# The first feed-forward block in Strassen's form, the bias tables in the mixer's projection, and a new order of vector work in the tails

## The reference

```python
def swiglu(x, w_gate, w_up, w_down):
    return (jax.nn.silu(x @ w_gate) * (x @ w_up)) @ w_down

for layer in range(DEPTH):
    g = norm_gains[layer]
    x = x + FFN_RESIDUAL * swiglu(rms_norm(x, g[0]), ffn_w_gate[layer, 0], ffn_w_up[layer, 0], ffn_w_down[layer, 0])
    xn = rms_norm(x, g[1])
    x = x + (dilated_pool_mixer(xn, rel_bias, ...) if layer % 2 == 0 else mlstm_mixer(xn, ...))
    x = x + FFN_RESIDUAL * swiglu(rms_norm(x, g[2]), ffn_w_gate[layer, 1], ...)
```

## Time and profile before

| | |
|---|---|
| median of 3 runs | 2024.57 us (2024.17 to 2025.17) |
| the profiled execution | 2022.4 us, of which its span is 2020.7 us |
| feed-forward 0 on PE | 10.15 to 377.95 us |
| even mixer | 377.95 to 563.13 us |
| feed-forward 1 | 563.13 to 911.77 us |
| feed-forward 2 | 911.77 to 1267.3 us |
| odd mixer | 1267.3 to 1669.4 us |
| feed-forward 3 | 1669.4 us to the end |
| busy: PE, DVE, ACT, POOL | 98%, 68%, 41%, 24% |

### The profile page before, as it was taken

How to read it: one execution, slowest core, us unless ns; L and a number is a source line. 1 busy time by engine, 2 the same in 40 slices (tenths; PEclk the granted TensorE clock), 3 DMA queues, 4 the chain that set the end, 5 groups by cost and what they waited for, 6 DMA issues and landing times.

```text
span 2020.7 us, 27444 instructions
## 1 busy us (share of the span) xinstructions
PE 1982.1 (98%) x11114; PEld 1701.4 (84%) x11114; DVE 1364.1 (68%) x1742; ACT 836.8 (41%) x1197; POOL 492.4 (24%) x358
## 2 busy tenths in 40 slices
PE   7999999999999999998999999999998999999999
PEld 6888888876789999987999998877775788999997
DVE  6333333545498888867888886784468857988884
ACT  5323223425563433345444334554545344433331
POOL 1202112133232211223221122254025512212211
PEclk9999999999999999999999999999999999999999
DMA  5233223421132323322333333222200133333323
GB/s 178 94 99 100 94 94 116 166 84 47 58 106 94 105 94 110 100 86 90 107 105 94 106 93 110 97 85 82 81 1 1 65 103 102 97 105 105 104 90 98
DMA packets 66377, 189.23 MB, mean 94 GB/s; under 512 B 6480, under 2 KB 14928, under 8 KB 66256
## 3 DMA queue, kind: packets, MB, share of 16 engines
q1 hardware_dynamic: 66256, 187.52, 28.8%
HBM read 182.78 MB, written 4.72 MB: 93 GB/s over the span
## 4 chain that ended last, share of the span: by engine, by line
PE 85%; DVE 9%; ACT 2%; issue 2%; POOL 1%; DMA 1%; SPq 0%; DVEq 0%; POOLq 0%; ACTq 0%
PE BANKS L538 13%; PE BANKS L539 13%; PE BANKS L540 13%; PE BANKS L626 9%; PE BANKS L628 9%; PE BANKS L627 9%; PE BANKS L676 4%; PE BANKS L677 4%; PE BANKS L678 4%; PE BANKS L970 1%; DVE LO L1546 1%; DVE LO L1457 1%; DVE XC L1858 1%; PE BANKS L798 1%; DVE SQ L1914 1%
## 5 line engine op out<-in xcount | busy, mean ns | idle before, releaser
L1457 DVE TENSOR_TENSOR LO<-RING,HI 128x1024 fp32r<-128x1024 f32 (+1 forms) x136 | 177.4, 1305 | 331.9 <-ACT HI L1032 331.8
L538 PE MATMUL BANKS<-XH,HI 128*128 128x512 f32 x896 | 352.4, 393 | 15.1 <-DVE XL L1466 15.0
L539 PE MATMUL BANKS<-XL,HI 128*128 128x512 f32 x896 | 350.3, 391 | 0.0
L540 PE MATMUL BANKS<-XH,LO 128*128 128x512 f32 x896 | 350.2, 391 | 0.0
L2063 POOL TENSOR_TENSOR TMP<-TMP,RSTD 128x512 f32<-128x512 f32 x66 | 101.4, 1537 | 625.3 <-ACT TMP L1126 625.3
L1032 ACT ACTIVATE HI<-RING 128x1024 fp32r<-128x1024 f32 (+1 forms) x144 | 150.1, 1043 | 216.5 <-DMA RING<-gu_dram 89.4
L538 PEld LDWEIGHTS BANKS<-XH,HI 128*128 128x128 f32 x896 | 169.3, 189 | 56.6 <-DVE LO L1457 11.0
L540 PEld LDWEIGHTS BANKS<-XH,LO 128*128 128x128 f32 x896 | 169.0, 189 | 35.8
L539 PEld LDWEIGHTS BANKS<-XL,HI 128*128 128x128 f32 x896 | 169.3, 189 | 34.5
L626 PE MATMUL BANKS<-BF,ASH 128*128 128x256 f32 x672 | 190.8, 284 | 4.0 <-DVE ASL L1573 3.9
L628 PE MATMUL BANKS<-BF,ASL 128*128 128x256 f32 x672 | 190.2, 283 | 0.0
(11 more groups left out here) (254 smaller groups left out, 4709.3 us busy)
## 6 DMA issues: line engine op xcount, KB each, us to landing
RING<-gu_dram SPq DMA_DIRECT2D x176, 512.0 KB, 3.4
DRAW<-down_dram SPq DMA_DIRECT2D x32, 512.0 KB, 3.8
RING<-oin_dram SPq DMA_DIRECT2D x32, 512.0 KB, 3.4
RING<-down_dram SPq DMA_DIRECT2D x32, 384.0 KB, 3.2
RING<-down_dram SPq DMA_DIRECT2D x16, 512.0 KB, 3.4
RING<-ein_dram SPq DMA_DIRECT2D x16, 512.0 KB, 3.4
RING<-oout_dram SPq DMA_DIRECT2D x16, 512.0 KB, 3.4
DRAW<-down_dram SPq DMA_DIRECT2D x16, 384.0 KB, 3.6
```

What stands on the lines that cost most here:

```text
L538: pe.matmul(PS[bank][:], HI[j][:, c], hi(k), start=(n == 0), stop=False)
L539: pe.matmul(PS[bank][:], HI[j][:, c], lo(k), start=False, stop=False)
L540: last = pe.matmul(PS[bank][:], LO[j][:, c], hi(k), start=False, stop=(n == len(order) - 1))
L1457: dve.tensor_tensor(LO[j][:, 0:kt * P], RAW[j][:, 0:kt * P], HI[j][:, 0:kt * P].bitcast(F32), ALU.subtract).then_inc(lo_ready, 1)
```

## The change

Feed-forward 0 is now a `block_ffn` as well, with `PLAIN` 4, `LATE` 6 and `EARLY` 16 as feed-forward 1 has them, so four plain pairs and 18 blocks; `ffn` and `walk_ffn` are gone. It begins with `start_of_program` in place of `start_of_stage`: units 0, 1, and unit 2 with the norm inside. Its forms are made right behind the start, the first of them ahead of the squares' low part. The bias tables move to the even mixer's input projection: heads 0 and 1 behind unit 3, then two heads behind each of the units 4, 5 and 6. Their table inputs `HOT` and `RELB` are loaded at the end of feed-forward 0; `STG` lies in two halves in another region, each half with a write of its own. In all the tails of `block_ffn` the low part of the weights of tile m - 1 stands between the add and the low part `XL` of tile m.

```diff
-PLAIN = (None, 4, 3, 3)
+PLAIN = (4, 4, 3, 3)
-LATE = (None, 6, 7, 7)
+LATE = (6, 6, 7, 7)
...
# SP
+                if f == 0:
+                    sp.wait_ge(early_done, EARLY)
+                    sp.dma_start(RELB[:], relb_d).then_inc(hot_in, 16)
+                    sp.dma_start(HOT[:], hot_d).then_inc(hot_in, 16)
+                    sp.dma_start(PICK[:], pick_d).then_inc(prep_in, 16)
+                    sp.dma_start(POOLW[:], poolw_d).then_inc(prep_in, 16)
...
-            ffn(0, Q_FFN[0], ein_d)
-
-            sp.wait_ge(skew_out, 16)
+            block_ffn(0, Q_FFN[0], ein_d)
+            for n in range(4, 11):
+                load(Q_EIN + n // 4, n % 4, ein_d[n if n < 8 else 8 + (n - 4) % 8])
+            for n in range(2):
+
+                sp.wait_ge(bias_staged, HA * (n + 1))
+                sp.dma_start(skew_d[4 * n:4 * n + 4].rearrange("h p z -> p h z"), STG[n][:]).then_inc(skew_out, 16)
+            for n in range(11, 13):
+                load(Q_EIN + n // 4, n % 4, ein_d[n if n < 8 else 8 + (n - 4) % 8])
+            sp.wait_ge(skew_out, 32)
...
# PE, start of the program and the even mixer
+            def start_of_program():
+
+                unit(0, 0, KX, xh, xl, ready=x_tile_ready(0))
+                unit(0, 1, KX, xh, xl)
+                unit_with_norm(0, 0)
...
                 start_of_stage(q0, 1)
                 unit(q0, 3, KX, xh, xl)
+                bias_table(0)
+                bias_table(1)
                 for j in range(SLOTS):
                     unit(q0 + 1, j, KX, xh, xl)
+                    if j < 3:
+                        bias_table(2 * j + 2)
+                        bias_table(2 * j + 3)
...
# ACT, even mixer
+                act.wait_ge(hot_in, 32)
+                act.activation(HOTR[:], HOT[:], ACT.Copy).then_inc(bias_ready, 1)
+                act.activation(RBH[:], RELB[:], ACT.Copy).then_inc(bias_ready, 1)
+
+                def staged(h):
+                    for n, (z0, z1) in ((2 * h, (0, T)), (2 * h + 1, (T, BW))):
+                        act.wait_ge(bias_sum, n + 1)
+                        act.activation(STG[h // 4][:, h % 4, z0:z1], PS[5 + n % 3][:, 0:z1 - z0],
+                                       ACT.Copy).then_inc(bias_staged, 1)
+
                 for n in range(12):
                     if n < 8:
                         act.wait_ge(bank_free, N_EIN + n + 5)
                         act.activation(SQB[:, n, :], QK[:, n, :], ACT.Square).then_inc(qk_sq, 1)
                     split_unit(N_EIN + n + 4)
+                    if 3 <= n <= 6:
+                        staged(2 * n - 6)
+                        staged(2 * n - 5)
...
# DVE, tails
-                for m in range(KX):
-                    residual_tile(q0 + (NU + m) // 4, m % 4, r, m, 0.5)
+
+                def split_behind(m):
                     if m < 4:
                         split(NU + 4 + m, late)
                     elif after:
                         split(NU + 4 + m, whole)
+
+                for m in range(KX):
+                    residual_add(q0 + (NU + m) // 4, m % 4, m, 0.5)
+                    if 1 <= m < KX - 1:
+                        split_behind(m - 1)
+                    if after:
+                        new_x_tile(r, m)
                     if f == 1:
                         forms_behind(2, m)
+                split_behind(KX - 2)
+                split_behind(KX - 1)
```

More of the change, by code:

```diff
@@ L196, in trunk @@
         HL = at("HL", [P, 8, T], hr0, 8 * TB, F32R)
[L198 to L201, removed]
+        STG = [at(f"STG{n}", [P, HA // 2, BW], hr0, 8 * n * TB) for n in range(2)]
+        HOT = at("HOT", [P, BW], hr0, 6 * TB)
+        HOTR = at("HOTR", [P, BW], hr0, 6 * TB, F32R)
+        RELB = at("RELB", [P, HA], hr0, 15 * TB // 2)
         QK = at("QK", [P, 8, T], e0, 0)
@@ L376, in early_loads @@
         def early_loads(f, p):
-            before = sum(len(early_pieces(i, n)) for i in range(1, f) for n in range(PLAIN[i], PLAIN[i] + EARLY))
+            before = sum(len(early_pieces(i, n)) for i in range(f) for n in range(PLAIN[i], PLAIN[i] + EARLY))
             return before + sum(len(early_pieces(f, n)) for n in range(PLAIN[f], p + 1))
@@ L383, in x_order @@
         def x_order(r):
-            return PAIRED if r >= 3 else tuple(range(KX))
+            return tuple(range(KX)) if r in (0, 2) else PAIRED
         NU = 2 * FT
-        def is_gate_up(lq, last):
-            return lq < (3 if last else 4)
         block = ctx.enter_context(nc.Block())
@@ L406, in load_half @@
                              src[:, :, first:first + 4 * P].rearrange("m p c -> p m c")).then_inc(weights_in[j], 16)
[L408 to L420, removed]
-                            load(q, j, gu_d[f, 32 + 4 * (lq + 1) + j] if lq + 1 < 3
-                                 else down2_d[f, 4 * (lq - 2) + j])
-                        elif lq + 1 < 4:
-                            load(q, j, gu_d[f, third * 16 + (4 * (lq + 1) + j)])
-                        elif lq + 1 < 6:
-                            load(q, j, down_d[f, third * 8 + (4 * (lq - 3) + j)])
-                        else:
-                            load(q, j, gu_d[f, third * 16 + (16 + j)])
-                walk_ffn(sp, step)
             def block_ffn(f, q0, after):
@@ L1642, in block_ffn @@
                 whole, right = slice(0, KMAX * P), slice(4 * P, KMAX * P)
-                now, first, late = (2, 3, 5)[f - 1], PLAIN[f], slice(0, LATE[f] * P)
-                if f == 1:
+                now, first, late = GAIN_OF[f], PLAIN[f], slice(0, LATE[f] * P)
+                if f < 2:
                     form(f, 0)
```

169 lines of the change are left out of this document (35 added, 134 removed).

## The result

The changed kernel takes 2042.66 us (2041.89 to 2044.69) against 2024.37 us (2021.57 to 2025.17) of the kernel before: a ratio of 1.0094, with a 95% interval of 1.0077 to 1.0112. The forecast was 2037 us, from 2030 to 2045. The profiled execution of the changed kernel takes 2042.0 us with a span of 2040.3, so it is 19.6 us longer than that of before.

A forecast was written before the change was run, and what follows sets the result against it. PE, busy 98% of the span, was taken to bound the kernel by its work plus waits. Terms -13.9 + 5.6 + 20.4 + 5.0 - 4.4 = +12.7 on 2022.4 gave 2035.1, with the median 2.2 above: 2037 us, range 2030 to 2045.

The forecast's parts named there:

- Blocks and start: Feed-forward 0: 18 blocks save 14.4 us, the start costs 2.9; -13.9 us in all, including 5.6 of bias tables leaving.
- The wait at the norm: Start of feed-forward 0: PE waits 0.8 us for the norm's sums, because the first form precedes the squares' low part.
- The loads of the tables' inputs: About 1.1 MB loaded ahead of the mixer's first weights: costed at nothing, up to 2 us if the cover is gone.
- The form by itself: Feed-forward 0 in Strassen's form, without the leaving bias tables: a gain of 8.3 us.
- Table waits: Mixer's projection: bias parts wait for ACT's copies, 7.8 us behind unit 3, 4.2 behind units 4, 5, 6; +20.4 us.
- Bias matmuls: The bias tables' matmuls leave feed-forward 0 and come back in the even mixer: +5.6 us.
- The clock: Even mixer: PE's granted clock falls in the 7.8 us wait and most 4.2 us ones; +5 us, between 1.7 and 7.
- The tail: Feed-forward 1's tail in the new order: the 4.35 us wait at feed-forward 2's start shrinks; -4.4 us, between 0 and -6.1.
- Rival 1: Table waits as forecast, but the clock falls once and the tail gives 6.1: +7.7, 2032 us; chance 0.85 together with the forecast.
- Rival 2: Mixer's projection: copies keep up with PE, so bias parts find banks free; -12.7, 2012 us; chance 0.06.
- Rival 3: Feed-forward 0: DVE stays behind, up to 5 us, clock falls there and at each table wait (+4); some 2046 us; chance 0.06.

The follow-up runs named there:

- four banks: Bias parts in four banks instead of three, with ACT's copies ahead of the square and split, against the changed kernel: 2012.16 us, ratio 0.9942.
- the copies first: Changed kernel with only ACT's copies of the bias parts moved ahead of the square and the weights' split: 2019.82 us, ratio 0.998 to the kernel before.
- the filled waits: Changed kernel with 33 unused matmuls put into PE's first table wait and 17 into each of the others: 2034.07 us, ratio 1.0053.
- one form moved: Four banks and copies ahead, with the one-piece form and its split moved behind feed-forward 0's norm, the last form further back: 2011.62 us, ratio 0.9939.

## Why the prediction was nearly right, step by step

The sign, the place and the mechanism were right. The time was 5.7 us too low by the medians. By the profiled execution it was 2042.0 - 2035.1 = 6.9: 5.2 in the mixer, 1.3 in feed-forward 0 and 0.4 in the tail. (The 2.2 us by which the median was to lie above the profiled execution were 0.7.) Most of it is one term, the clock.

- **Blocks and start, forecast -13.9, measured -12.6.** A block in feed-forward 0 starts at 109.95 and the next piece at 120.02, so it takes 10.07 us, as in the earlier trace rows. By an estimate from the Trainium skill's pace ("TensorE: Matmul & The Clock Gate", section "Wait — 56ns, not 53.3ns?") the stage would have gained some 6.8 us more; that pace does not hold for these fp32r matmuls, and the rows decide.

```profile
109.95 0.28 PE L581 MATMUL BANKS<-XH,HI 128*128 128x256 f32 x1
...
120.02 0.40 PE L631 MATMUL BANKS<-HH,DHI 128*128 128x512 f32 x1
```

The start went as worked out: the norm's sums wait 0.6 (forecast 0.8), the fifth unit starts at 38.05 (38.0). In the timeline of DVE the form (24.13 to 25.66) stands ahead of the squares' low part, and the first scaling (L1502) ends at 37.9:

```profile
24.13 0.48 DVE L1437 SCALAR_TENSOR_TENSOR BFR<-X,PAR,MID 128x256 f32<-128x256 f32 x1
...
25.66 0.68 DVE L1416 TENSOR_TENSOR SQL<-SQ,SQH 128x512 fp32r<-128x512 f32 x1
...
37.22 0.68 DVE L1502 TENSOR_TENSOR TMP<-BANKS,RSTD 128x512 f32<-128x512 f32 x1
```
```profile
26.49 0.47 PE L558 MATMUL BANKS<-SQH,SELR 128*128 128x512 f32 x1 [0.60 <-DVE SQL L1416]
...
38.05 0.47 PE L514 MATMUL BANKS<-XH,HI 128*128 128x512 f32 x1 [2.01 <-DVE TMP L1502]
```

The wait at the norm is worth nothing by itself: with four banks PE was a little ahead and waited 1.8 us there, and its fifth unit came at 37.79, 27.85 us after its first matmul as in the changed kernel. DVE sets that moment. The loads of the tables' inputs, which the prediction cost at nothing, did cost nothing: PE has no wait from the mixer's start to the first bias part. The form by itself was to bring 8.3 us, and the kernel with the old tail, four banks and the copies first is 7.9 us faster than before.

What I left out is that the clock can fall behind these 2.0 us as well. Six kernels have this same start. In four of them (the changed one, the copies first, the filled waits, the old tail) the clock falls behind the wait, and the stage takes 355.1 to 355.4 us. In the two with four banks and the new tail it doesn't, and the stage takes 353.9. The difference is 1.3 us, as much as the forecast of the stage was off. The rest of the stage behind the fifth unit's start takes 327.3 us in the changed kernel and 326.1 with four banks; the forecast was 326.0. The windows, first of the changed kernel, then of the one with four banks and the copies first:

```profile
38.00:43.00 5.00, 4.95 (x15) 0.66 0.20 80
```
```profile
40.00:44.00 4.00, 4.00 (x19) 1.00 0.01 2
```

- **Table waits, forecast +20.4, measured +20.0.** Four waits, released by ACT's `STG`, forecast at 7.8 and three times 4.2; the rows have 7.46, 3.96, 3.88 and 4.72. The working holds in its parts too: the split was to begin 3.64 us after the unit and began 3.67 after (408.15 - 404.48), the bank was to be free 5.3 after and was 5.27 after.

```profile
396.42 0.47 PE L570 MATMUL BANKS<-HOTR,RBH 128*128 128x128 f32 x1 [7.46 <-ACT STG L1157]
...
423.15 0.47 PE L570 MATMUL BANKS<-HOTR,RBH 128*128 128x128 f32 x1 [3.88 <-ACT STG L1157]
...
437.51 0.47 PE L570 MATMUL BANKS<-HOTR,RBH 128*128 128x128 f32 x1 [4.72 <-ACT STG L1157]
```

- **Bias matmuls, forecast +5.6.** The kernel with four banks has them without a wait: 190.8 - 185.2 = 5.6.

- **The clock, forecast +5.0 within 1.7 to 7, measured about +9.9.** This is the term that failed, and nearly all of the miss. From the mixer's 36.2 us, 5.6 of matmuls and some 20.7 of waits (measured from start to start) leave 9.9; filling the waits gave back 9.4. That the clock falls at every wait was the upper end of the forecast, and true. The size was wrong: I took 1.7 us from the earlier trace rows, where the lower level lasted 3.4 us, and took it three to four times. Here it lasted about 10 us around the first wait and 7 around the end of each of the others. Over the 7 us behind each of the four waits the granted clock is 0.65, 0.63, 0.61 and 0.66, so 2.4 to 2.7 us are lost each time, 10.1 in all, and a unit there took 7.5 to 7.9 us, not 5.44. One fall in one profile isn't a price. The end of the range should have been four units at the lower pace for most of their length, by these rows 4 x 2.3 = 9 us, and not four times the one duration seen.

- **The tail, forecast -4.4 within 0 to -6.1, measured -4.0** in the stage, and 3.9 by the experiment with the old tail. The add of tile 7 was to be 7.2 us after the stage's start and is 7.14 after (942.37 - 935.23). The wait of 4.35 is 0.36, and the fifth unit waits, as the prediction had it, because DVE has one more low part to do ahead of the forms:

```profile
942.37 0.69 DVE L1431 SCALAR_TENSOR_TENSOR X<-BANKS,X 128x512 f32<-128x512 f32 x1
```
```profile
946.91 0.50 PE L514 MATMUL BANKS<-XH,HI 128*128 128x512 f32 x1 [0.36 <-DVE LO L1465]
...
959.75 0.47 PE L514 MATMUL BANKS<-XH,HI 128*128 128x512 f32 x1 [1.16 <-DVE TMP L1502]
```

- **The rivals.** Rival 1, the clock falling once, had a place (the kernel with the copies first shows one fall), but not in this kernel. Rival 2, the copies keeping up, was priced at 2012 us, and that is what the kernel with four banks takes, 2012.16: the price was right and its condition was not met, since the wait is one of order. Rival 3 was wrong in its place: behind the fifth unit feed-forward 0 has no wait above 1 us. Its extra 4 us of clock at the table waits, though, are what happened; I had tied them to a mechanism with which they have nothing to do, and gave it 0.06.

The best kernels, with four banks and the copies first, are faster than the kernel before: 2012.16 us against 2023.16 in the same comparison, and with one form moved 2011.62 against 2024.38.

## What to carry to other kernels

When work that goes through a small ring of buffers is moved, look for the release that now stands behind another instruction on the copying engine: two table parts more per unit turned a ring of three banks into a wait behind each of four units, and one bank more, or the copy written first, or both, took 24 to 31 us back. A long wait of PE costs more than its length. Behind the eight waits of 3.9 to 7.5 us in these profiles (the program's start left out) the clock was low each time, and the loss, read from the granted clock over the 7 us behind, was 1.6 us in before, 1.7 with the copies first, and 2.4 to 2.9 in the six others. So a range should reach to the larger value for each wait. Where DVE is busy almost throughout up to a deadline, moving its work mostly moves the wait, and a move can break up the hand-over between two engines and cost more.

## What the runs showed of the hardware that was not expected

The length of a low stretch of the clock isn't set by the wait ahead of it alone. The wait of 4.4 us at the start of feed-forward 2 was followed by 3.4 us at 1.2 GHz in before and by 7 in the kernel with the old tail. The wait of 2.0 us at the fifth unit was followed by a fall in four kernels and by none in two, with the same code up to there. The odd mixer's waits of 1.9 and 2.6 us, in code that no kernel here touches, are followed by low stretches that differ in number and length from profile to profile, and the mixer's time goes with them: 402.1 us with one stretch of 3.4 us, 403.5 to 403.9 with two of these or one of twice the length, 405.2 with three, 406.0 with two of some 7 us. In the changed kernel, of one stretch:

```profile
1575.00:1580.00 5.00, 4.37 (x17) 0.66 0.01 3
```

It doesn't take an edit: the eleven runs of the kernel with the new tail alone lie 4.5 us apart, and the slower a run, the lower its granted clock, from 1.000 down to 0.997. So two kernels that differ in nothing but an edit elsewhere can come out 4 us apart in one profile, and a stage must be compared with the same stage, with the granted clock beside it. What sets the number and the length stays open: the long waits of the cases above are the same and in the same order. It was not tried whether filling the odd mixer's waits would keep its clock up, as it did in the even one.
